# A decoder trunk on one core: the first rows, the first token tile and the first weight block in smaller steps

## What is computed

```python
for i in range(DEPTH):
    x = x + 0.5 * swiglu(rmsnorm(x, ln_ff1[i]), w_ff1_in[i], w_ff1_out[i])
    h = rmsnorm(x, ln_mix[i])
    ...
    x = x + 0.5 * swiglu(rmsnorm(x, ln_ff2[i]), w_ff2_in[i], w_ff2_out[i])
return rmsnorm(x, ln_final)
```

## Time and profile before

| | |
|---|---|
| Median of 3 runs | 956.91 us (955.53 to 957.76) |
| Profiled execution, span from first to last instruction | 952.5 us |
| TensorE busy | 937.7 us (98%) |
| DVE busy | 542.6 us (57%) |
| ACT busy | 440.6 us (46%) |
| POOL busy | 28.2 us (3%) |
| Mean transfer rate | 177 GB/s |
| Mean granted TensorE clock of the core | 0.997 |

### The profile page before, as it was taken

One profiled execution on the slowest core, in us unless ns is written; L12 is line 12 of the kernel. 1 busy time (PEld: TensorE's weight loads), 2 busy tenths in 40 slices (PEclk: granted clock), 3 DMA queues, 4 the chain that ended last, 5 costly groups with the idle time before them and its releaser, 6 DMA issues.

```text
span 952.5 us, 12737 instructions
## 1 busy us (share of the span) xinstructions
PE 937.7 (98%) x4363; PEld 774.3 (81%) x4363; DVE 542.6 (57%) x646; ACT 440.6 (46%) x615; POOL 28.2 (3%) x55
## 2 busy tenths in 40 slices
PE   7999999999999999999999999999999999999997
PEld 6888888888888888888888888888778888888885
DVE  5754554568656545545575454556866574554534
ACT  6553444456435534444354443534565473444432
POOL 1000000000000000000000000000411000000000
PEclk9999999999999999999999999999999999999999
DMA  8756474447644664656456566563440196465631
GB/s 277 255 186 212 147 223 158 155 154 266 221 146 156 189 216 150 213 166 201 145 197 205 180 198 199 162 218 106 156 154 16 48 318 215 151 215 164 199 109 44
DMA packets 122100, 168.81 MB, mean 177 GB/s; under 512 B 8589, under 2 KB 98773, under 8 KB 122069
## 3 DMA queue, kind: packets, MB, share of 16 engines
q1 hardware_dynamic: 121936, 168.35, 54.7%
q10 hardware_dynamic: 132, 0.04, 0.0%
HBM read 167.31 MB, written 1.05 MB: 177 GB/s over the span
## 4 chain that ended last, share of the span: by engine, by line
PE 94%; DVE 1%; DMA 1%; ACT 1%; POOL 1%; issue 1%; SPq 0%; ACTq 0%; DVEq 0%; POOLq 0%
PE acc L1090 30%; PE proj L1074 19%; PE proj L1076 19%; PE proj L1075 19%; PE tp L1134 2%; PE tp L1125 1%; PE tp L1140 1%; DMA raw_in<-in_w_ff_in 1%; PE proj L1272 1%; PE acc L1272 1%; POOL scratch L395 1%; PE acc L1298 1%; PE tp L1298 1%; DVE in_lo L703 0%; ACT gated L457 0%
## 5 line engine op out<-in xcount | busy, mean ns | idle before, releaser
L1074 PE MATMUL proj<-in_hi,xT_hi 128*128 128x512 f32 x848 | 336.9, 397 | 1.0 <-DVE xT_lo L758 0.6
L1076 PE MATMUL proj<-in_hi,xT_lo 128*128 128x512 f32 x848 | 331.4, 391 | 0.0
L1075 PE MATMUL proj<-in_lo,xT_hi 128*128 128x512 f32 x848 | 330.9, 390 | 0.0
L703 DVE TENSOR_TENSOR in_lo<-raw_in,in_hi 128x1024 fp32r<-128x1024 f32 x212 | 251.0, 1224 | 43.5 <-ACT in_hi L420 43.3
L420 ACT ACTIVATE in_hi<-raw_in 128x1024 fp32r<-128x1024 f32 x212 | 212.7, 1051 | 15.7 <-PE proj L1076 6.2
L464 ACT ACTIVATE gated<-proj,rstd 128x256 f32<-128x256 f32 x88 | 41.6, 473 | 363.7 <-PE proj L1076 363.7
L766 DVE SCALAR_TENSOR_TENSOR gated<-proj,rstd,gated 128x256 f32<-128x256 f32 x88 | 42.6, 484 | 274.5 <-ACT gated L464 274.3
L1074 PEld LDWEIGHTS proj<-in_hi,xT_hi 128*128 128x128 f32 x848 | 159.6, 188 | 35.2 <-issue 1.3
L1076 PEld LDWEIGHTS proj<-in_hi,xT_lo 128*128 128x128 f32 x848 | 159.6, 188 | 34.2
L1075 PEld LDWEIGHTS proj<-in_lo,xT_hi 128*128 128x128 f32 x848 | 159.9, 189 | 31.6
L710 DVE TENSOR_TENSOR out_lo<-raw_out,out_hi 128x1024 fp32r<-128x1024 f32 x96 | 114.2, 1230 | 6.1 <-ACT out_hi L428 6.1
(11 more groups left out here) (102 smaller groups left out, 468.4 us busy)
## 6 DMA issues: line engine op xcount, KB each, us to landing
raw_in<-in_w_ff_in SPq DMA_DIRECT2D x352, 256.0 KB
raw_out<-in_w_ff_out SPq DMA_DIRECT2D x88, 512.0 KB, 5.4
raw_in<-in_conv_w_in SPq DMA_DIRECT2D x24, 512.0 KB
raw_in<-in_attn_w_qkv SPq DMA_DIRECT2D x12, 512.0 KB
raw_out<-in_conv_w_out SPq DMA_DIRECT2D x8, 512.0 KB, 5.4
raw_out<-in_attn_w_o SPq DMA_DIRECT2D x8, 512.0 KB, 3.3
x<-in_x SPq DMA_DIRECT2D x2, 512.0 KB, 4.6
scratch<-in_ln_final SPq DMA_DIRECT2D x1, 512.0 KB, 4.2
```

The source lines that it names most:

```text
L703: dve.tensor_tensor(in_lo[:, slot, 2 * q:2 * q + 2, :], raw_in[:, 2 * q:2 * q + 2, :], in_hi[:, slot, 2 * q:2 * q + 2, :].bitcast(F32), AL ...
L1074: pe.matmul(proj[t][:, :], x_hi, in_hi[:, slot, k, :], start=(k == 0), stop=False)
L1075: pe.matmul(proj[t][:, :], x_hi, in_lo[:, slot, k, :], start=False, stop=False)
L1076: last = pe.matmul(proj[t][:, :], x_lo, in_hi[:, slot, k, :], start=False, stop=(k == KD - 1))
```

## The change

Four things, all at the start:

1. The 16 rows of `ln_ff1` get a tile and a semaphore of their own, `first_rows`. TensorE transposes them ahead of the token tile and DVE copies these 16 columns at once. The 56 other rows are transposed after tile 0's matmuls of block 0, into an accumulator bank that is still free, and copied by DVE just ahead of `hidden` of tile 0.
2. Token tile 0 is loaded in two halves of 512 columns. The transposes of each half wait for their own half. The order on SP is now: half 0 of the tile, k tile 0 of the weights, half 1 of the tile, k tile 1, piece 1, and on as before.
3. Piece 0 of block 0 is loaded and split k tile by k tile (four instructions of 128x512 for two of 128x1024), between the halves of `pair`, `xT_hi` and `xT_lo` of tile 0. The matmuls of k 0 wait for k tile 0 alone.
4. The 18 warm-up transposes become 6 before the first rows are waited for and 8 behind the transposes of token tile 0.

```diff
-WARM_UP = 18
+WARM_UP = (6, 8)
+FIRST_ROWS = 2 * KD
...
-        rows = sb("rows", [GAIN_ROWS + CONV_ROWS, P])
+        first_rows = sb("first_rows", [FIRST_ROWS, P])
+        rows = sb("rows", [GAIN_ROWS + CONV_ROWS - FIRST_ROWS, P])
...
-            sp.dma_start(x[:, 0, :], x_in[0, 0:P, :]).then_inc(x_landed[0], 16)
-            load_in(0, 0, 0, F, (0, 1))
+            sp.dma_start(x[:, 0, 0:W], x_in[0, 0:P, 0:W]).then_inc(x_half_landed, 16)
+            first = w_in[0].rearrange("(k p) (g n) -> p k g n", p=P, g=2)
+            for k in range(2):
+                sp.dma_start(raw_in[:, k, :].rearrange("p (g n) -> p g n", g=2), first[:, k, :, 0:UNIT]).then_inc(
+                    first_k_landed if k == 0 else in_landed[0], 16 if k == 0 else 32)
+                if k == 0:
+                    sp.dma_start(x[:, 0, W:D], x_in[0, 0:P, W:D]).then_inc(x_landed[0], 16)
+            load_in(0, 0, 0, F, (1,))
             sp.dma_start(x[:, 1, :], x_in[0, P:2 * P, :]).then_inc(x_landed[1], 16)
...
-            for n, g in enumerate(gains):
+            act.dma_start(first_rows[:, :], gains[0].rearrange("l (k p) -> (l k) p", p=P)).then_inc(first_rows_landed, 16)
+            for n, g in enumerate(gains[1:]):
...
-            split_in(0, 0, (0,))
-            norm_hi(0, 0)
+            act.wait_ge(first_k_landed, 16)
+            act.activation(in_hi[:, 0, 0, :], raw_in[:, 0, :], ACT.Copy).then_inc(first_k_hi, 1)
+            norm_hi(0, 0, (0,))
+            act.wait_ge(in_landed[0], 32)
+            act.activation(in_hi[:, 0, 1, :], raw_in[:, 1, :], ACT.Copy).then_inc(in_hi_done, 1)
+            norm_hi(0, 0, (1,))
             split_in(0, 0, (1, 2, 3))
...
-            dve.tensor_copy(cols[:, :], proj[1][:, 0:GAIN_ROWS + CONV_ROWS]).then_inc(cols_ready, 1)
+            dve.tensor_copy(cols[:, 0:FIRST_ROWS], proj[1][:, 0:FIRST_ROWS]).then_inc(cols_ready, 1)
             dve.wait_ge(cols_ready, 1)
-            norm_gain(0, 0)
-            split_in(0, 0, (0,))
-            norm_rest(0, 0)
+            norm_gain(0, 0, (0,))
+            dve.wait_ge(first_k_hi, 1)
+            dve.tensor_tensor(in_lo[:, 0, 0, :], raw_in[:, 0, :], in_hi[:, 0, 0, :].bitcast(F32),
+                              ALU.subtract).then_inc(first_k_lo, 1)
+            norm_rest(0, 0, (0,))
+            norm_gain(0, 0, (1,))
+            dve.wait_ge(in_hi_done, 1)
+            dve.tensor_tensor(in_lo[:, 0, 1, :], raw_in[:, 1, :], in_hi[:, 0, 1, :].bitcast(F32),
+                              ALU.subtract).then_inc(in_lo_done, 1)
+            norm_rest(0, 0, (1,))
...
                     split_in(u + 1, (u + 1) % 2, (0, 1))
+                    if s == 0:
+                        dve.wait_ge(cols_ps, 2)
+                        dve.tensor_copy(cols[:, FIRST_ROWS:GAIN_ROWS + CONV_ROWS],
+                                        acc[0][1][:, 0:GAIN_ROWS + CONV_ROWS - FIRST_ROWS]).then_inc(cols_ready, 1)
+                        dve.wait_ge(cols_ready, 2)
                     hidden(c, 0)
...
-                    if (fresh or first and t == 0) and k % 2 == 0:
+                    if first and t == 0 and m == 0 and k < 2:
+                        pe.wait_ge(first_k_lo if k == 0 else in_lo_done, 1)
+                    elif (fresh or first and t == 0) and k % 2 == 0:
...
-                        pe.wait_ge(x_landed[t], 16)
+                        pe.wait_ge(x_half_landed if t == 0 and half == 0 else x_landed[t], 16)
...
+            for _ in range(WARM_UP[0]):
+                pe.transpose(acc[0][0][:, 0:P], ident[:, :], ident[:, :])
+            pe.wait_ge(first_rows_landed, 16)
+            pe.transpose(proj[1][:, 0:FIRST_ROWS], first_rows[:, :], ident[0:FIRST_ROWS, 0:FIRST_ROWS]).then_inc(cols_ps, 1)
             transpose_x(0, 0)
-            pe.wait_ge(rows_landed, 16 * (len(gains) + 1))
-            n_rows = GAIN_ROWS + CONV_ROWS
-            pe.transpose(proj[1][:, 0:n_rows], rows[:, :], ident[0:n_rows, 0:n_rows]).then_inc(cols_ps, 1)
-            for _ in range(WARM_UP):
+            for _ in range(WARM_UP[1]):
                 pe.transpose(acc[0][0][:, 0:P], ident[:, :], ident[:, :])
...
+                if s == 0:
+                    pe.wait_ge(rows_landed, 16 * len(gains))
+                    n_rows = GAIN_ROWS + CONV_ROWS - FIRST_ROWS
+                    pe.transpose(acc[0][1][:, 0:n_rows], rows[:, :], ident[0:n_rows, 0:n_rows]).then_inc(cols_ps, 1)
+                    pe.wait_ge(cols_ready, 1)
                 project(m, u, 1, u % 2, first=True)
+                if s == 0:
+                    pe.wait_ge(cols_ready, 2)
```

More of the change, by code:

```diff
@@ L207, in build @@
         x_landed = [sem(f"x_landed{t}") for t in range(NT)]
+        first_rows_landed = sem("first_rows_landed")
         rows_landed = sem("rows_landed")
+        x_half_landed = sem("x_half_landed")
+        first_k_landed = sem("first_k_landed")
+        first_k_hi = sem("first_k_hi")
+        first_k_lo = sem("first_k_lo")
         pos_landed = sem("pos_landed")
@@ L439, in split_late_out, with norm_hi @@
                                    raw_out[:, h, :].rearrange("p (k n) -> p k n", k=2), ACT.Copy).then_inc(out_hi_done, 1)
-            def norm_hi(m, t):
-                for half in range(2):
+            def norm_hi(m, t, halves=(0, 1)):
+                for half in halves:
                     act.wait_ge(gained, 4 * m + 2 * t + half + 1)
@@ L451, in squares @@
                     act.wait_ge(x_landed[t], 16)
+                    if t == 0:
+                        act.wait_ge(x_half_landed, 16)
                 else:
@@ L470, in hidden_hi @@
                                ACT.Copy).then_inc(hT_hi_done, 1)
-            for n, g in enumerate(gains):
+            act.dma_start(first_rows[:, :], gains[0].rearrange("l (k p) -> (l k) p", p=P)).then_inc(first_rows_landed, 16)
+            for n, g in enumerate(gains[1:]):
                 act.dma_start(rows[n * 2 * KD:(n + 1) * 2 * KD, :],
                               g.rearrange("l (k p) -> (l k) p", p=P)).then_inc(rows_landed, 16)
-            act.dma_start(rows[GAIN_ROWS:GAIN_ROWS + CONV_ROWS, :],
+            act.dma_start(rows[GAIN_ROWS - FIRST_ROWS:GAIN_ROWS - FIRST_ROWS + CONV_ROWS, :],
                           conv_kernel[0].rearrange("w (k p) -> (w k) p", p=P)).then_inc(rows_landed, 16)
             rstd_col = [None]
-            split_in(0, 0, (0,))
-            norm_hi(0, 0)
+            act.wait_ge(first_k_landed, 16)
[4 more added lines that the diff above has]
+            norm_hi(0, 0, (1,))
             split_in(0, 0, (1, 2, 3))
@@ L740, in norm_lo, with norm_gain @@
                 norm_rest(m, t)
-            def norm_gain(m, t):
-                for half in range(2):
+            def norm_gain(m, t, halves=(0, 1)):
+                for half in halves:
                     n = 4 * m + 2 * t + half
@@ L750, in norm_gain, with norm_rest @@
                                       gain_of(m, half), ALU.mult).then_inc(gained, 1)
-            def norm_rest(m, t):
-                for half in range(2):
+            def norm_rest(m, t, halves=(0, 1)):
+                for half in halves:
                     n = 4 * m + 2 * t + half
```

## The result

The changed kernel is slower by a quarter of a per cent: 958.15 us (median of 12 runs, 955.43 to 960.66) against 955.53 (12 runs of the kernel before), a ratio of 1.0026 with a 95% interval of 1.0013 to 1.0038. Five more rounds on one chip gave 956.83 against 955.82, a ratio of 1.0012 (1.0001 to 1.0023). The two intervals overlap between 1.0013 and 1.0023, that is 1.2 to 2.2 us. The forecast was no change.

What follows compares the result with a forecast made beforehand. Loaded volume was taken to bound the start (3.18 MB at 346 GB/s). First matmul -1.8, given back +1.8, copy 0, transfers 0: from 956.9 us, a tenth lower for the transfer bounds, 956.8; range 954.9 to 958.3.

Steps and rivals of the forecast that it cites:

- The chain: Opening: landing of piece 3 (block 0's last k tiles) at 11.94, then ACT and DVE, set block 1 at 22.72.
- The work parts: Opening: first matmul 1.8 us earlier, given back at pieces 2 and 3 and block 1's wait; 56-column copy hidden, 0.
- An earlier landing of piece 3: Rival, opening loads: piece 3 lands 0.3 to 1.3 us earlier, block 1 moves along, giving 955.6 to 956.6; chance 0.16.
- the transfer term: Opening loads: same bytes ahead, so piece 3 lands at 11.94 again; 0 us, between -1.3 and +0.4.
- "above": Upper bound for the opening loads: half the token rows per packet and more DMAs cost 0 to +0.4 us.
- The first rows: Start of TensorE's work: the 16 `ln_ff1` rows land at 4.4 us; up to about 4.8 costs nothing.
- The clock rival: TensorE's opening: fewer warm-ups and new idle times halve the clock; 957.6 for one fall, 963.3 if long; chance 0.07.
- 0.88 on no change: Whole kernel: chance 0.88 that the time stays within about 0.2%, 1.9 us; faster 0.07, slower 0.05.

Runs made afterwards that it cites:

- b_new_moves: The kernel before with only the change's transfers (token tile 0 in halves, piece 0 by k tile, alternating): 955.89 against 955.52 us, ratio 1.0012.
- b_all_k: The kernel before with all four weight pieces of block 0 loaded by k tile: piece 3's split at 12.98 us, block 1 at 23.71; one profiled execution.
- a_whole_tile: The changed kernel with token tile 0 in one transfer, piece 0 still by k tile: piece 3's split at 12.58 us, in the second execution (_2) 12.28.
- a_halves_2: Second profiled execution of the changed kernel with both halves of token tile 0 loaded first, then piece 0 by column half: piece 3's split at 13.10 us.
- a_old_moves: The changed kernel with the transfers of token tile 0 and piece 0 as in the kernel before: 956.11 against 956.05 us, ratio 0.9999.
- a_halves_first: The changed kernel with both halves of token tile 0 loaded first, then piece 0 by column half, first execution: piece 3's split at 12.63 us.
- best_pieces: The changed kernel with old transfers, tile 0's squares early on ACT, piece 0 split whole: 954.92 against 955.82 us, ratio 0.9995; again (_2) 0.9997.
- a_columns: The changed kernel with token tile 0 in halves, alternating with piece 0 by column half instead of k tile: piece 3's split at 12.87 us.
- repeat_after: The changed kernel profiled once more, nothing altered, for the spread: piece 3's split at 13.34 us, block 1 at 24.17.
- b_last_k: The kernel before with only piece 3, the last two transfers of block 0, by k tile: piece 3's split at 11.89 us; one profiled execution.

## Why the prediction was wrong

**The chain was right.** From piece 3's split to block 1 it is 10.7 to 10.9 us in all kernels that keep ACT's order, with one exception: 11.98 to 22.72, 11.93 to 22.66 (before), 13.51 to 24.35, 13.34 to 24.17, 13.63 to 24.46 (after), 13.73 to 24.45 (`b_new_moves`), 12.98 to 23.71 (`b_all_k`), 12.28 to 23.12 (`a_whole_tile_2`). The exception is `a_halves_2`, 13.10 to 24.77, where TensorE's clock fell (below). The chain of waits, led back through ACT and DVE to that one transfer, held to 0.1 us in the others.

**The work parts were right in what they give, not in their room.** The early first rows and the finer splits give nothing once the transfers are the old ones (0.9999), and what was won at the first matmul is given back at k 2, as the text said. The copy of 56 columns is hidden but for about 0.1: block 1 follows piece 3 by 10.84 instead of 10.74. But TensorE was to be through block 0 at 22.0 and to wait 0.7 for `gated`. In `a_old_moves` k 2 starts at 11.70 and not at 11.25, the last matmul at 22.48, and nothing of the 0.7 is left. An earlier landing of piece 3, which the prediction took to be worth up to 0.7 by itself, would have moved block 1 by next to nothing.

**The step that failed is the transfer term.** It said: the same bytes, so piece 3 lands at 11.94 again; "above", +0.4; "I take 0". Measured: 1.4 to 1.8 us later, at piece 3 and at block 1. The reasoning that failed is "the start is bound by the volume that is loaded". A mean rate of 346 GB/s and a share of 1.01 from 2 to 12 us say what the engines do with the transfers as they were. They don't say that the same bytes move at that rate in another form. The volume was the same, and the form of the first four transfers alone took the rate of the first 7 us from 299 to 236 GB/s and put piece 3 at 13.34 to 13.73.

**Why the form costs stays open.** The obvious reading is that the engines run out of work: one issue of 0.38 us put 0.52 MB in the queue, 1.5 us of work at 346 GB/s, and a half tile is only 0.26 MB. The numbers don't bear it out as the whole cause. 0.26 MB are 0.75 us of work, and the next issue starts 0.62 to 0.70 after the last, so by this sum the queue fills faster than it empties. The share falls (0.87 to 0.76), but the rate falls more; with the k tiles alone the share doesn't fall at all (0.88 and 0.91). Nor are slow transfers wherever they stand the answer for the k tiles, since piece 3 in that form cost nothing. What the runs show is the price of each form at the start, not its mechanism. The +0.4 was taken from the mean of transfers in the old form; no row of the kernel before had a price for the new one.

**The sentence on the page.** The Trainium skill, DMA: Bandwidth & Descriptors, Specifications, puts a core's share of HBM at about 358 GB/s; it was weighed only as to whether the loads could be faster. The measured loss lies far below this figure, at 161 GB/s from 3 to 4 us, so it doesn't bear on the miss.

**The first rows** had landed by 3.09, some 2.3 us after the issue, and not at 4.4: the estimate came from a load 64 times as large and from one issued behind three others. It had no effect, since nothing on the way to piece 3 waits for them.

**The clock rival** had the right place and no price in the changed kernel. The profile prints 1.00 there, but the pace says that the first matmuls ran at the lower level: starts 0.43 apart until 9.66, 11.19 and 12.17 in the three executions, where those of the kernel before come every 0.23 from the second on. Piece 3's chain hid it, 10.83 to 10.84 each time. A fall that the profile prints came in four other executions, each after TensorE had been idle for 2.03 to 3.13 us ahead of its first matmuls: `a_halves_first`, `a_halves_2`, `best_pieces` and `best_pieces_2`. (Idle times of 2.06 to 2.45 between the two rounds of token transposes, at 4 to 7 us in `a_columns` and `repeat_after`, were followed by no printed fall.) In `a_halves_2` (idle 2.03) the granted clock is 0.50 (1.2 GHz) from 10 us on:

```profile
9.00:10.00 1.00, 1.00 (x3) 0.33 (x3) 0.90 (x3) 0.93 (x2) 0.00 (x0) 0.53 1.08 382
10.00:11.00 1.00, 1.00 (x3) 0.52 (x2) 0.74 (x2) 0.64 (x1) 0.00 (x0) 0.50 1.10 384
```

There the second tile's transposes came so late that ACT's wait for `pair` grew from 1.89 to 2.33, and TensorE itself was last: block 1 is 11.67 behind piece 3 instead of 10.8.

**The size.** The price of the miss is the 1.4 to 1.8 us of the opening. That the median of 958.15 lies inside the stated range is luck: the range was justified by other mechanisms and by the spread of three runs, and 0.88 on no change was too sure for a sum that rested on one unmeasured 0.

## What to carry to other kernels

At a start that waits for its loads, splitting the first transfers to let compute begin sooner can delay everything queued behind them, with the same bytes on the same queue: here by 1.4 to 1.8 us for four transfers. A mean rate over the opening doesn't price another form, and neither does comparing a transfer's bytes with the length of an issue, which here would have said that nothing is lost. Build the version with only the transfers changed and read the last landing that the chain waits for. The first matmul can come 1.7 us earlier and change nothing.

## What the runs showed of the hardware

- The same 0.26 MB of weights took 0.55 to 0.65 us to issue as one k tile with two column groups (`after`, `b_new_moves`), and 0.42 to 0.43 as two k tiles of one group (`a_columns`). Both have 256 runs of 1 KB in memory.
- That form cost 0.4 to 0.7 us as the first two weight transfers and nothing beyond the spread as the last two of the block (`b_last_k`).
- The transfer engines' share and their rate can part: from 3 to 4 us 0.91 of the time gave 167 GB/s (`repeat_after`) and 0.98 gave 357 (`before`).
- A transfer can be seen to land 2 us late though the total moved by 8 us is nearly the same (`best_pieces`, 2.07 for 2.09 MB). A stretch at 72 GB/s and a share of 0.25 stood ahead of the landing; the cause is open.
- A wait of TensorE for POOL in the attention stage is 2.2 us in nine executions and 3.2 to 3.3 in eight, whatever the kernel; in one (`a_whole_tile`) it is 1.33.
